# An attention and MLP block in split float32: seven-product pairs moved to tiles 4 and 10, totals taken one bank at a time

## The chip, the cores and the metric

The kernel runs on one core of a Trainium2 chip. The metric is the device time of one execution in microseconds (us); of several timed runs the median counts. Engines: TensorE (PE, its weight loads PEld), VectorE (DVE), ScalarE (ACT), GpSimd (POOL) and SyncE (SP, which issues the weight transfers).

## The reference, cut to what matters

One transformer block on 256 tokens of width 2048 in float32. The stages around the change:

```python
h = h + (g_mla * y_mla + g_fox * y_fox) @ w_out[l]
hn = rmsnorm(h, mlp_norm[l])
u = jnp.square(jax.nn.relu(hn @ w_up[l]))      # 2048 -> 8192
h = h + u @ w_down[l]                          # 8192 -> 2048
return rmsnorm(h, final_norm)
```

Before them come one combined input projection, latent attention and forgetting attention, which the change leaves alone.

## The kernel before, in words

**Split products.** Each float32 operand is held as a high part (rounded to the format that TensorE multiplies) and a low part (the rest). A product is three matmuls into one PSUM bank: high x high, high x low, low x high (`three_passes`, L695 to L699). Every matmul has a 128 x 128 stationary block and 512 moving columns. The activations are stationary, the weights moving.

**The weight stream.** All weights arrive as 456 units of 128 x 1024 (512 KB) in the order of use. A ring of four slots holds them raw, another ring of four holds the high and low parts. For unit u SyncE issues the load when unit u-4 has been split (L521); ScalarE rounds it to the high part when TensorE has used unit u-4 (L941, `unit_used`); VectorE subtracts to get the low part (L1190, `unit_split`). ScalarE and VectorE take units strictly in order, and between units the other work that the list `DUE` puts there (`make_due`, L186). `due[u]` is worked off after unit u has been split. A wait in one such piece of work holds all later units on that engine.

**The up product.** `w_up` is taken in two parts of 4096 columns; each part is an up stage (four groups) and a down stage (four groups). A group of the up stage gives 1024 hidden columns (two chunks of 512) for both blocks of 128 tokens: 16 tiles of depth 128, one unit each, into four banks (bank 2c + tb for chunk c and token block tb). An ordinary tile is 4 x 3 matmuls. Two pairs of tiles in each group are done by seven products in place of eight (`seven_products`, L709), as in Strassen's scheme: sums of activations (`sums_hl`) times sums of weights (`wsum_hi`, `wsum_lo`) and plain blocks. Four of the seven go to banks 4 to 7, three directly to banks 1, 0 and 2. `SEVEN = (0, 6)` names the first tile of each pair, so the pairs are tiles 0, 1 and 6, 7. Before splitting the pair's first unit VectorE forms the weight sums out of both raw units (L1200, L1203, L1204), ScalarE rounds them (L946, L948) and VectorE subtracts (L1207). The sums of activations are made once, from the turned and scaled rows of w_out's chunks 0 and 1 (`row_sums`, L1210).

**What follows a group.** ScalarE copies bank 4 (`copy_p1`, due at tile 10) and VectorE sums the four products into `hid` (`sum_products`, three operations, due at tile 11). The last two tiles of a group are done bank by bank, so bank 0 is complete first. `totals` (L1236, due two units after the group) adds banks 0 and 1 one at a time and banks 2 and 3 in one operation. `hidden_squares` does ReLU and square on ScalarE for each chunk (L1007, L1009; due 3 and 4 units after the group). `turn_hidden` transposes each chunk in blocks of 32 on VectorE (L1385; due 4 and 6 units after) into the one buffer `blocks`; GpSimd stores that to HBM and loads it back in four transfers (L545, L552). A transpose waits until the transfer before it has been stored. The chunks that come back are split (L1022, L1405; due 13 and 15 units after).

**TensorE's waits at the start of a group.** The pair at tile 0 first writes banks 7, 5, 6 and 4, in twelve matmuls, then waits for banks 0 and 1 to be free, later for banks 2 and 3. Where the group before in those banks is w_out's or down's, "free" means that VectorE has added it to the residual (`resid_done`; L1456 for w_out, L1461 for down). w_out's last chunk is due at tile 2 of part 0's first group, down's last at tile 3 of part 1's first group. In the list for tile 2 the scaling of w_out's chunk 2 (`turned_times_gains`, L1396) stands ahead of the residual addition.

The text calls the tiles of a group k0 to k15 and the two halves of the MLP part 0 and part 1.

Of the kernel before, what the change touches and what calls it, by code (L numbers as in the profile page):

```python
# [74 lines left out]
        self.name, self.g = name, g  # L75


SEVEN = (0, 6)
SUMS = {k: n for n, k in enumerate(SEVEN)}


def make_groups():
# [103 lines left out]
def make_due():  # L186


    due = [[] for _ in range(N_UNITS)]

    def after(unit, what, g):
        due[min(unit + RING, N_UNITS - 1)].append((what, g))

    for gr in GROUPS:
        middle = gr.u0 + gr.units // 2 - 1
        if (gr.name, gr.g) in SCORES_IN:
            after(middle, "scored", SCORES_IN[gr.name, gr.g])
        if gr.name == "y_fox" and gr.g >= 2:
            after(middle, "mixed", 4 + gr.g)
        if gr.name[:2] == "up":  # L200
            due[gr.u0 + 10].append(("p1 copied", gr))
            due[gr.u0 + 11].append(("products summed", gr))
            due[gr.last + 2].append(("totals", gr))
            for c in range(2):
                piece = Chunk(gr.name, 2 * gr.g + c)
                piece.of, piece.c = gr, c
                due[gr.last + 3 + c].append(("hidden", piece))
                due[gr.last + 4 + 2 * c].append(("hidden turns", piece))
                due[gr.last + 13 + 2 * c].append(("u turned", piece))
            continue  # L210
        if gr.name in ("y_mla", "w_out"):
            if gr.name == "w_out":
                after(gr.last + TURN_UNITS["w"] - 1, "h back", gr)
            after(gr.last + TURN_UNITS[gr.name[0]], {"y": "m turned", "w": "h turned"}[gr.name[0]], gr)
        if gr.name == "fq" and gr.g == 0:
            for later, what in ((2, "x norm"), (3, "latent norms"), (6, "keys rotated"), (9, "cq back"),
                                (10, "cq turned"), (14, "keys back"), (15, "keys turned"), (17, "forget exp"),
                                (18, "forget sums")):
                after(gr.u0 + later, what, gr)
        if gr is GROUPS[-1]:  # L220
            continue
        later = {("fq", 0): 5, ("fq", 1): 4, ("ukv_k", 0): 2, ("w_out", CHUNKS - 1): -1}.get((gr.name, gr.g), 0)
        after(gr.last + later - (gr.units == 1), "group", gr)
        if gr.name == "gates" and gr.g < 4:
            after(gr.last, "mixed", gr.g)
        elif gr.name == "gates" and gr.g == 7:
            after(gr.last, "mixed", 4)
        elif gr.name == "y_fox" and gr.g == 0:
            after(gr.last, "mixed", 5)
        elif gr.name in ("fq", "uq_nope"):  # L230
            after(gr.last + later + 8, "queries turned", gr)
        elif gr.name == "uq_rope":
            after(gr.last + 8, "queries rotated", gr)
# [51 lines left out]
def program(nc, stream, x_t, x_n, consts, gains, final_gain, cum_rows, prob_rows, turn_rows, out_n):  # L285
# [83 lines left out]
    with ctx:  # L369
# [260 lines left out]
        def _(pe):  # L630
            def wait_for_banks(gr):
# [2 lines left out]
                if had is None:  # L634
                    return
                if had.name[:2] == "up":
                    pe.wait_ge(totals_done, 3 * had.n + (2 if gr.pair == 0 else 3))
# [63 lines left out]
            def double_group(gr, tile, before_unit):  # L701
# [4 lines left out]
                def weights(k, c):  # L706
                    return lambda part: hl[:, slot_of(gr.unit[k]), part, c * WIDE:c * WIDE + WIDE]

                def seven_products(k):  # L709

                    n, one = SUMS[k], SUMS[k] == 0
# [5 lines left out]
                    if one:  # L717
                        pe.wait_ge(products_summed, gr.n)
                    pe.wait_ge(wsum_split, 2 * SEVEN_AT[gr.u0 + k] + 1)
                    three_passes(7, sum_rows(2), sum_weights(1), one, last)  # L720
                    three_passes(5, sum_rows(0), sum_weights(0), one, last)
                    pe.wait_ge(wsum_split, 2 * SEVEN_AT[gr.u0 + k] + 2)
                    three_passes(6, sum_rows(1), sum_weights(2), one, last)
                    pe.wait_ge(unit_split, gr.unit[k] + 1)
                    three_passes(4, rows(k, 0), weights(k, 0), one, last).then_inc(seven_summed, 1)
                    if one:
                        if gr.before.name == "w_out":
                            pe.wait_ge(resid_done, RESID0["w_out"] + gr.before.g + 1)
                        elif gr.before.name[:2] == "up":
                            pe.wait_ge(totals_done, 3 * gr.before.n + 2)  # L730
                        else:
                            pe.wait_ge(resid_done, RESID0[gr.before.name] + gr.before.g + 1)
                    three_passes(1, rows(k + 1, 1), weights(k, 1), one, False).then_inc(unit_used, 1)
                    pe.wait_ge(unit_split, gr.unit[k + 1] + 1)
                    three_passes(0, rows(k + 1, 0), weights(k + 1, 1), one, False)
                    if one:
                        if gr.before_right.name[:2] == "up":
                            pe.wait_ge(totals_done, 3 * gr.before_right.n + 3)
                        else:
                            pe.wait_ge(resid_done, RESID0[gr.before_right.name] + gr.before_right.g + 1)  # L740
                    three_passes(2, sum_rows(3), weights(k + 1, 0), one, False).then_inc(unit_used, 1)

                BANKS = [(0, 0), (1, 0), (0, 1), (1, 1)]
                k = 0
                while k < gr.units - 2:
# [4 lines left out]
                        continue  # L750
                    pe.wait_ge(unit_split, gr.unit[k] + 1)
                    for tb, c in BANKS:
                        done = three_passes(2 * c + tb, rows(k, tb), weights(k, c), (k, tb, c) == (2, 1, 1), False)
                    done.then_inc(unit_used, 1)
                    k += 1
                before_unit(k)
                for tb, c in BANKS:
                    for i in range(k, gr.units):
                        pe.wait_ge(unit_split, gr.unit[i] + 1)
                        done = three_passes(2 * c + tb, rows(i, tb), weights(i, c), False, i == gr.units - 1)  # L760
                    if c == 0:
                        done.then_inc(block_left, 1)
                done.then_inc(unit_used, 2)

# [147 lines left out]
        def _(act):  # L912
# [89 lines left out]
            def hidden_squares(piece):  # L1002

                d, c = piece.of.n, piece.c
                act.wait_ge(totals_done, 3 * d + 2 + c)
# [88 lines left out]
            for u in range(N_UNITS):  # L1094
# [4 lines left out]
                for what, g in DUE[u]:  # L1099
# [25 lines left out]
                        forget_exp()  # L1125
                    elif what in ("m turned", "h turned", "u turned"):
                        turned_to_hi(g)
                        if what == "h turned" and g.g < len(SEVEN):
                            row_sums_to_hi(g.g)
                    elif what == "p1 copied":  # L1130
                        copy_p1(g)
                    elif what == "hidden":
# [27 lines left out]
        def _(dve):  # L1160
# [48 lines left out]

            def row_sums(gr):  # L1210

                n, back = gr.g, by_token(turned[:, SPLIT_NO[gr.name, gr.g] % 2])
# [23 lines left out]
            def totals(gr):  # L1236

                dve.wait_ge(products_summed, gr.n + 1)
                dve.wait_ge(block_left, 2 * gr.n + 1)
                nc.vector.tensor_tensor(hid[:, 1], bank[:, 0], hid[:, 1], ALU.add).then_inc(totals_done, 1)  # L1240
                dve.wait_ge(block_left, 2 * gr.n + 2)
                nc.vector.tensor_tensor(hid[:, 2], bank[:, 1], hid[:, 2], ALU.subtract).then_inc(totals_done, 1)
                dve.wait_ge(unit_used, gr.last + 1)
                nc.vector.tensor_tensor(hid[:, 3:5], bank[:, 2:4], hid[:, 3:5], ALU.add).then_inc(totals_done, 1)  # L1244

            def turn_hidden(piece):

# [230 lines left out]
            for u in range(N_UNITS):  # L1478
# [4 lines left out]
                for what, g in DUE[u]:  # L1483
# [35 lines left out]
                        turn_blocks(g, query_rows[:].rearrange("p b h r -> p b (h r)"))  # L1519
                    elif what == "h back":  # L1520
                        turned_times_gains(g)
                        if g.g < len(SEVEN):
                            row_sums(g)
                    elif what in ("m turned", "h turned", "u turned"):
                        turned_to_lo(g)
                        if what == "h turned" and g.g < len(SEVEN):
                            row_sums_to_lo(g.g)
# [94 lines left out]
```

## Time and profile before

| | |
|---|---|
| timed runs, median of 3 | 1294.25 us (1293.98 to 1296.37) |
| profiled execution, its own time | 1288.84 us |
| its span, first to last instruction | 1287.0 us |
| TensorE busy | 1262.4 us, 98% |
| TensorE weight loads busy | 1043.5 us, 81% |
| VectorE busy | 848.8 us, 66% |
| ScalarE busy | 640.6 us, 50% |
| GpSimd busy | 138.0 us, 11% |
| granted TensorE clock, mean | 0.998 |
| chain that ended last | TensorE 78%, VectorE 11%, transfers 6%, issue 2%, ScalarE 2% |

Matmuls overlap: a record of 512 columns lasts 389 ns, yet one starts about every 227 ns while the engine has work. A gap between two starts is therefore longer by about 0.16 us than the idle time in the record. The first matmuls after a gap are a little slower too: the second starts some 0.34 us after the first.

### The profile page before, as it was taken

How to read it: one execution, taken by the hardware profiler on the slowest of the kernel's cores; microseconds unless marked ns; L12 is line 12 of the kernel's file. 1: busy time of each engine (PE TensorE's matmuls, PEld its weight loads, DVE VectorE, ACT ScalarE, POOL GpSimd, SP SyncE). 2: the span in 40 equal slices, each digit the busy share in tenths (PEclk: the TensorE clock that was granted, in tenths of full speed). 3: DMA queues.
4: the chain of work that ended last, by engine and by line, in shares of the span. 5: the costliest groups of instructions: out<-in, count | busy, mean ns of one | idle time of the engine just before them, and what ended most of it. 6: DMA issues, size and time to landing. Idle time of an engine off the chain costs nothing.

```text
span 1287.0 us, 14484 instructions
## 1 busy us (share of the span) xinstructions
PE 1262.4 (98%) x5618; PEld 1043.5 (81%) x5618; DVE 848.8 (66%) x889; ACT 640.6 (50%) x748; POOL 138.0 (11%) x239
## 2 busy tenths in 40 slices
PE   9999999999999999999999999999999999999997
PEld 7888888888888888877877778888888877788886
DVE  6676567546776676688888775444667887654544
ACT  6654345444555444445555654333445556453443
POOL 0122001004211111100101110000001011100000
PEclk9999999999999999999999999999999999999999
DMA  9698756756976788767678777666566767866563
GB/s 338 238 306 281 243 181 218 222 191 205 286 237 213 241 271 265 247 194 239 215 232 245 246 231 239 192 194 192 192 196 213 242 226 253 286 203 212 195 190 123
DMA packets 83141, 293.90 MB, mean 228 GB/s; under 512 B 11320, under 2 KB 12416, under 8 KB 82432
## 3 DMA queue, kind: packets, MB, share of 16 engines
q1 hardware_dynamic: 67536, 243.04, 57.9%
q0 software_dynamic: 14528, 48.00, 12.2%
q10 hardware_dynamic: 1008, 1.92, 0.4%
q8 instruction: 45, 0.74, 0.2%
q14 instruction: 24, 0.20, 0.0%
HBM read 269.45 MB, written 23.47 MB: 228 GB/s over the span
## 4 chain that ended last, share of the span: by engine, by line
PE 78%; DVE 11%; DMA 6%; issue 2%; ACT 2%; POOL 0%; DVEq 0%; POOLq 0%; ACTq 0%
PE bank L651 65%; DVE hl L1190 4%; PE bank L697 4%; PE bank L699 3%; PE bank L698 3%; DMA raw<-weights 3%; DMA turn_rows<-blocks 2%; DVE wsum_lo L1207 1%; ACT hl L941 1%; DVE wsum L1200 1%; DVE blocks L1385 1%; DVE wsum L1203 1%; DVE raw L1204 1%; PE bank L822 1%; ACT hid L1007 0%
## 5 line engine op out<-in xcount | busy, mean ns | idle before, releaser
L1190 DVE TENSOR_TENSOR hl<-raw,hl 128x1024 fp32r<-128x1024 f32 x451 | 547.2, 1230 | 364.4 <-ACT hl L941 364.3
L941 ACT ACTIVATE hl<-raw 128x1024 fp32r<-128x1024 f32 x451 | 470.5, 1056 | 477.0 <-PE bank L651 376.8
L651 PE MATMUL bank<-hl,u_hl 128*128 128x512 f32 x1536 | 348.8, 389 | 2.6 <-DVE hid L1244 2.6
L651 PE MATMUL bank<-hl,x_hl 128*128 128x512 f32 (+1 forms) x1536 | 344.8, 385 | 0.0
L651 PEld LDWEIGHTS bank<-hl,u_hl 128*128 128x128 f32 x1536 | 288.1, 188 | 63.3 <-DVE hid L1244 3.5
L651 PEld LDWEIGHTS bank<-hl,x_hl 128*128 128x128 f32 x1536 | 284.1, 188 | 56.7 <-DVE hl L1181 0.4
L697 PE MATMUL bank<-hl,hn_hl 128*128 128x512 f32 x432 | 168.9, 391 | 4.5 <-DVE resid L1456 3.2
L699 PE MATMUL bank<-hl,hn_hl 128*128 128x512 f32 x432 | 168.1, 389 | 0.0
L698 PE MATMUL bank<-hl,hn_hl 128*128 128x512 f32 x432 | 168.1, 389 | 0.0
L697 PEld LDWEIGHTS bank<-hl,hn_hl 128*128 128x128 f32 x432 | 81.1, 188 | 24.1 <-DVE resid L1456 3.7
L699 PEld LDWEIGHTS bank<-hl,hn_hl 128*128 128x128 f32 x432 | 81.1, 188 | 17.0
L698 PEld LDWEIGHTS bank<-hl,hn_hl 128*128 128x128 f32 x432 | 81.1, 188 | 16.6
L651 PE MATMUL bank<-hl,m_hl 128*128 128x512 f32 x384 | 87.4, 389 | 0.0
L651 PEld LDWEIGHTS bank<-hl,m_hl 128*128 128x128 f32 x384 | 72.0, 188 | 15.2 <-DVE hl L1190 0.3
L545 POOL DMA_DIRECT2D turn_rows<-blocks x35 | 19.7, 564 | 567.0 <-DVE blocks L1385 566.7
L552 POOL DMA_DIRECT2D turned<-turn_rows x96 | 52.7, 555 | 100.7 <-DMA turn_rows<-blocks 95.9
L946 ACT ACTIVATE wsum_hi<-wsum 128x1024 fp32r<-128x1024 f32 x16 | 17.0, 1062 | 75.2 <-DVE wsum L1200 75.2
L651 PE MATMUL bank<-hl,o_fox 128*128 128x512 f32 x192 | 45.1, 392 | 0.0
L651 PE MATMUL bank<-hl,o_mla 128*128 128x512 f32 x192 | 43.7, 389 | 0.0
L651 PEld LDWEIGHTS bank<-hl,o_mla 128*128 128x128 f32 x192 | 36.0, 188 | 7.5
L651 PEld LDWEIGHTS bank<-hl,o_fox 128*128 128x128 f32 x192 | 35.6, 188 | 7.3
L969 ACT ACTIVATE prob<-prob,cols 128x128 f32<-128x128 f32 (+1 forms) x32 | 14.2, 444 | 31.9 <-DVE cols L1352 31.9
(188 smaller groups left out, 786.3 us busy)
## 6 DMA issues: line engine op xcount, KB each, us to landing
raw<-weights SPq DMA_DIRECT2D x454, 512.0 KB, 4.3
turn_rows<-blocks POOLq DMA_DIRECT2D x34, 512.0 KB, 3.7
turned<-turn_rows POOLq DMA_DIRECT2D x96, 128.0 KB, 4.9
prob_rows<-prob_blocks POOLq DMA_DIRECT2D x8, 384.0 KB, 2.7
prob_t<-prob_rows POOLq DMA_DIRECT2D x32, 96.0 KB, 5.8
turned_h<-turn_rows POOLq DMA_DIRECT2D x20, 128.0 KB, 4.6
x_rows<-x_n POOLq DMA_DIRECT2D x2, 1024.0 KB, 9.0
resid<-x_n POOLq DMA_DIRECT2D x1, 2048.0 KB, 8.2
```

What stands on the lines that cost most here:

```text
L545: pool.dma_start(turn_rows[n % 2, :, 0:4 * run], blocks[:, 0:4 * run]).then_inc(blocks_stored, 16)
L552: pool.dma_start(back[32 * q:32 * q + 32].rearrange("p a k b j -> p a (k b j)"), turn_rows[n % 2, :, run * q:run * q + run].rearrange("(a ...
L651: return nc.tensor.matmul(bank[:, gr.pair + tb, 0:gr.cols], tile[:, k, x_part, tb * P:tb * P + P], w, start=k == 0 and not x_part and not ...
L697: nc.tensor.matmul(bank[:, to], rows(0), w(0), start=first, stop=False)
L698: nc.tensor.matmul(bank[:, to], rows(0), w(1), start=False, stop=False)
L699: return nc.tensor.matmul(bank[:, to], rows(1), w(0), start=False, stop=last)
L822: nc.tensor.matmul(bank[:, 6, hh * T:hh * T + T], v[:, 0, cs], prob_t[n % 2][:, :, hh, 0:2].rearrange("p a k j -> p k a j"), start=True, s ...
L941: nc.scalar.activation(hl[:, slot, 0], raw[:, slot], ACT.Copy).then_inc(unit_hi, 1)
L946: nc.scalar.activation(wsum_hi[:, 0:2], wsum[:, 0:2], ACT.Copy).then_inc(wsum_rounded, 1)
L969: nc.scalar.activation(prob[:, hh, piece], prob[:, hh, piece], ACT.Exp, bias=cols[:, 1, c:c + 1], accum_out=cols[:, 2, c:c + 1]).then_inc( ...
L1190: nc.vector.tensor_tensor(hl[:, slot, 1], raw[:, slot], hl[:, slot, 0].bitcast(F32), ALU.subtract).then_inc(unit_split, 1)
L1200: nc.vector.tensor_tensor(wsum[:, 0:2], raw[:, a, WIDE:].unsqueeze(1).broadcast_to([P, 2, WIDE]), raw[:, a:b + 1, 0:WIDE], ALU.add).then_i ...
```

## The change

- The pairs of seven products are tiles 4, 5 and 10, 11 instead of 0, 1 and 6, 7. Their row sums now come from w_out's chunks 1 and 2 (`IN_CHUNK`).
- The copy of bank 4 and the summing of the products are due at tiles 14 and 15 instead of 10 and 11.
- TensorE waits for each bank at its first use in a group, through `begin`, which also sets the matmul's start flag.
- `totals` adds each of the four banks by itself, each when it is complete; `totals_done` counts four for a group instead of three, and `block_left` three instead of two.
- The hidden chunks' ReLU and square are due one unit earlier (2 and 3 units after the group). The transposes are due 3 and 7 units after it instead of 4 and 6, so that four units lie between the two. The splits of what comes back are due 12 and 15 units after instead of 13 and 15.

The core of the diff:

```diff
-SEVEN = (0, 6)
+SEVEN = (4, 10)
 SUMS = {k: n for n, k in enumerate(SEVEN)}
+IN_CHUNK = {k // 4: n for n, k in enumerate(SEVEN)}
...
-            due[gr.u0 + 10].append(("p1 copied", gr))
-            due[gr.u0 + 11].append(("products summed", gr))
+            due[gr.u0 + SEVEN[-1] + 4].append(("p1 copied", gr))
+            due[gr.u0 + SEVEN[-1] + 5].append(("products summed", gr))
             due[gr.last + 2].append(("totals", gr))
...
-                due[gr.last + 3 + c].append(("hidden", piece))
-                due[gr.last + 4 + 2 * c].append(("hidden turns", piece))
-                due[gr.last + 13 + 2 * c].append(("u turned", piece))
+                due[gr.last + 2 + c].append(("hidden", piece))
+                due[gr.last + 3 + 4 * c].append(("hidden turns", piece))
+                due[gr.last + 12 + 3 * c].append(("u turned", piece))
...
+                def begin(to):
+
+                    first = to not in begun
+                    begun.add(to)
+                    if first and to >= 4:
+                        pe.wait_ge(products_summed, gr.n)
+                    elif first:
+                        had = (gr.before, gr.before_right)[to // 2]
+                        if had.name[:2] == "up":
+                            pe.wait_ge(totals_done, 4 * had.n + to + 1)
+                        else:
+                            pe.wait_ge(resid_done, RESID0[had.name] + had.g + 1)
+                    return first
...
-                        done = three_passes(2 * c + tb, rows(i, tb), weights(i, c), False, i == gr.units - 1)
-                    if c == 0:
+                        done = add_to(2 * c + tb, rows(i, tb), weights(i, c), i == gr.units - 1)
+                    if 2 * c + tb < 3:
                         done.then_inc(block_left, 1)
...
-                        if what == "h turned" and g.g < len(SEVEN):
-                            row_sums_to_hi(g.g)
+                        if what == "h turned" and g.g in IN_CHUNK:
+                            row_sums_to_hi(IN_CHUNK[g.g])
...
-                dve.wait_ge(block_left, 2 * gr.n + 1)
+                dve.wait_ge(block_left, 3 * gr.n + 1)
                 nc.vector.tensor_tensor(hid[:, 1], bank[:, 0], hid[:, 1], ALU.add).then_inc(totals_done, 1)
-                dve.wait_ge(block_left, 2 * gr.n + 2)
+                dve.wait_ge(block_left, 3 * gr.n + 2)
                 nc.vector.tensor_tensor(hid[:, 2], bank[:, 1], hid[:, 2], ALU.subtract).then_inc(totals_done, 1)
+                dve.wait_ge(block_left, 3 * gr.n + 3)
+                nc.vector.tensor_tensor(hid[:, 3], bank[:, 2], hid[:, 3], ALU.add).then_inc(totals_done, 1)
                 dve.wait_ge(unit_used, gr.last + 1)
-                nc.vector.tensor_tensor(hid[:, 3:5], bank[:, 2:4], hid[:, 3:5], ALU.add).then_inc(totals_done, 1)
+                nc.vector.tensor_tensor(hid[:, 4], bank[:, 3], hid[:, 4], ALU.add).then_inc(totals_done, 1)
```

## Rows read from the trace of the kernel before

**Rows 1.** Windows: length, then PE, PEld, DVE, ACT, POOL busy (count), clock, DMA share, GB/s
```profile
755.49:929.70 174.21, 174.21 (x768) 144.26 (x769) 92.04 (x80) 74.86 (x72) 5.50 (x10) 1.00 0.63 202
...
1105.63:1279.80 174.17, 174.17 (x768) 144.07 (x768) 89.62 (x84) 77.69 (x87) 5.51 (x10) 1.00 0.62 199
```

**Rows 2.** Timeline of PE: start, duration in us, instruction, count [idle before <- releaser]
```profile
1.32 4.54 PE L846 MATMUL bank<-kr_low 128*128 128x256 f32 x10 [1.32 <-POOL kr_low L534]
...
572.70 1.07 PE L651 MATMUL bank<-hl,m_hl 128*128 128x512 f32 x4
574.60 0.47 PE L697 MATMUL bank<-wsum_hi,sums_hl 128*128 128x512 f32 x1 [0.83 <-DVE wsum_lo L1207]
...
580.85 0.50 PE L697 MATMUL bank<-hl,hn_hl 128*128 128x512 f32 x1 [3.25 <-DVE resid L1456]
...
755.49 0.73 PE L651 MATMUL bank<-hl,u_hl 128*128 128x512 f32 x2 [1.32 <-DVE hid L1244]
...
933.62 0.50 PE L697 MATMUL bank<-hl,hn_hl 128*128 128x512 f32 x1 [1.01 <-DVE resid L1461]
...
1033.46 0.47 PE L697 MATMUL bank<-wsum_hi,sums_hl 128*128 128x512 f32 x1 [2.11 <-DVE wsum_lo L1207]
```

**Rows 3.** Waits of PE over the span: us in total, times, longest
```profile
PE bank L697 <- DVE wsum_lo L1207: 9.2, 6, 2.7
```

**Rows 4.** Timeline of DVE from a group's end to its second pair
```profile
1016.13 0.68 DVE L1240 TENSOR_TENSOR hid<-bank,hid 128x512 f32<-128x512 f32 x1
...
1017.33 1.21 DVE L1244 TENSOR_TENSOR hid<-bank,hid 128x1024 f32<-128x1024 f32 x1
...
1021.72 1.24 DVE L1385 STREAM_TRANSPOSE blocks<-hid 128x1024 f32<-128x1024 f32 x1
...
1028.38 1.25 DVE L1385 STREAM_TRANSPOSE blocks<-hid 128x1024 f32<-128x1024 f32 x1 [2.45 <-DMA turn_rows<-blocks]
1029.54 1.18 DVE L1200 TENSOR_TENSOR wsum<-raw 128x1024 f32<-128x1024 f32 x1
...
1033.83 2.35 DVE L1190 TENSOR_TENSOR hl<-raw,hl 128x1024 fp32r<-128x1024 f32 x2
```

**Rows 5.** Timeline of ACT over the same group's ReLU and square
```profile
1017.44 1.06 ACT L1007 ACTIVATE hid<-hid 128x1024 f32<-128x1024 f32 x1 [0.64 <-DVE hid L1242]
1018.53 1.06 ACT L1009 ACTIVATE hid<-hid 128x1024 f32<-128x1024 f32 x1
1019.50 1.04 ACT L941 ACTIVATE hl<-raw 128x1024 fp32r<-128x1024 f32 x1
```

**Rows 6.** Timeline of DVE, the first of the three operations on the products
```profile
999.79 0.69 DVE L1230 TENSOR_TENSOR hid<-bank,hid 128x512 f32<-128x512 f32 x1
```

**Rows 7.** Timeline of DVE and ACT at the starts of part 0 and part 1
```profile
578.38 1.29 DVE L1396 TENSOR_TENSOR turned<-turned,gain 128x512 f32<-128x512 f32 x2
579.58 1.21 DVE L1456 TENSOR_TENSOR resid<-resid,bank 128x1024 f32<-128x1024 f32 x1
...
932.16 1.40 DVE L1461 SCALAR_TENSOR_TENSOR resid<-bank,rstd_col,resid 128x512 f32<-128x512 f32 x2
...
929.93 1.06 ACT L941 ACTIVATE hl<-raw 128x1024 fp32r<-128x1024 f32 x1 [1.66 <-PE bank L651]
```

**Rows 8.** DMA issues in 683.0:683.5, 674:676 and 563:567, count, KB, us to landing
```profile
raw<-weights SPq DMA_DIRECT2D x1, 512.0 KB, 3.5
...
raw<-weights SPq DMA_DIRECT2D x2, 512.0 KB, 5.8
...
raw<-weights SPq DMA_DIRECT2D x3, 512.0 KB, 8.6
```

**Rows 9.** One of the four row-sum operations: duration ns min/median/max, first and last start
```profile
L1216 DVE TENSOR_TENSOR sums<-turned x2: 292/293/294, 547.3 to 553.6; 128x128 f32<-128x128 f32 x2
```

**Rows 10.** Windows around the longest gap and after the last matmul
```profile
579.00:582.50 3.50, 1.65 (x7) 1.39 (x8) 3.04 (x4) 1.64 (x5) 0.00 (x0) 1.00 0.82 280
...
1280.10:1287.00 6.90, 0.00 (x0) 0.00 (x0) 3.00 (x8) 2.43 (x6) 0.00 (x0) 0.65 0.54 202
```

More of the change, by code:

```diff
@@ L636, in wait_for_banks @@
                 if had.name[:2] == "up":
-                    pe.wait_ge(totals_done, 3 * had.n + (2 if gr.pair == 0 else 3))
+                    pe.wait_ge(totals_done, 4 * had.n + gr.pair + 2)
                 elif had.name in ("keys", "fq") and gr.name[0] == "u":
@@ L707, in weights, with add_to @@
                     return lambda part: hl[:, slot_of(gr.unit[k]), part, c * WIDE:c * WIDE + WIDE]
+                begun = set()
+                def begin(to):
[10 more added lines that the diff above has]
+                    return first
+                def add_to(to, rows, w, last=False):
+                    return three_passes(to, rows, w, begin(to), last)
                 def seven_products(k):
-                    n, one = SUMS[k], SUMS[k] == 0
+                    n = SUMS[k]
                     last = n == len(SEVEN) - 1
@@ L716, in seven_products @@
                         pe.wait_ge(sums_split, n + 1)
-                    if one:
-                        pe.wait_ge(products_summed, gr.n)
                     pe.wait_ge(wsum_split, 2 * SEVEN_AT[gr.u0 + k] + 1)
-                    three_passes(7, sum_rows(2), sum_weights(1), one, last)
-                    three_passes(5, sum_rows(0), sum_weights(0), one, last)
+                    add_to(7, sum_rows(2), sum_weights(1), last)
+                    add_to(5, sum_rows(0), sum_weights(0), last)
@@ L722, in seven_products @@
                     pe.wait_ge(wsum_split, 2 * SEVEN_AT[gr.u0 + k] + 2)
-                    three_passes(6, sum_rows(1), sum_weights(2), one, last)
+                    add_to(6, sum_rows(1), sum_weights(2), last)
                     pe.wait_ge(unit_split, gr.unit[k] + 1)
[L725 to L732, printed above, removed]
@@ L733, in seven_products @@
-                    three_passes(1, rows(k + 1, 1), weights(k, 1), one, False).then_inc(unit_used, 1)
-                    pe.wait_ge(unit_split, gr.unit[k + 1] + 1)
[L735 to L740, printed above, removed]
@@ L741, in seven_products @@
-                    three_passes(2, sum_rows(3), weights(k + 1, 0), one, False).then_inc(unit_used, 1)
+                    add_to(4, rows(k, 0), weights(k, 0), last).then_inc(seven_summed, 1)
+                    add_to(1, rows(k + 1, 1), weights(k, 1)).then_inc(unit_used, 1)
+                    pe.wait_ge(unit_split, gr.unit[k + 1] + 1)
+                    add_to(0, rows(k + 1, 0), weights(k + 1, 1))
+                    add_to(2, sum_rows(3), weights(k + 1, 0)).then_inc(unit_used, 1)
                 BANKS = [(0, 0), (1, 0), (0, 1), (1, 1)]
@@ L752, in double_group @@
                     for tb, c in BANKS:
-                        done = three_passes(2 * c + tb, rows(k, tb), weights(k, c), (k, tb, c) == (2, 1, 1), False)
+                        done = add_to(2 * c + tb, rows(k, tb), weights(k, c))
                     done.then_inc(unit_used, 1)
@@ L1004, in hidden_squares @@
                 d, c = piece.of.n, piece.c
-                act.wait_ge(totals_done, 3 * d + 2 + c)
+                act.wait_ge(totals_done, 4 * d + 2 + 2 * c)
                 z = hid[:, 1 + 2 * c:3 + 2 * c]
@@ L1210, in row_sums @@
             def row_sums(gr):
-                n, back = gr.g, by_token(turned[:, SPLIT_NO[gr.name, gr.g] % 2])
+                n, back = IN_CHUNK[gr.g], by_token(turned[:, SPLIT_NO[gr.name, gr.g] % 2])
                 i = SEVEN[n] - 4 * gr.g
@@ L1521, in _ @@
                         turned_times_gains(g)
-                        if g.g < len(SEVEN):
+                        if g.g in IN_CHUNK:
                             row_sums(g)
@@ L1525, in _ @@
                         turned_to_lo(g)
-                        if what == "h turned" and g.g < len(SEVEN):
-                            row_sums_to_lo(g.g)
+                        if what == "h turned" and g.g in IN_CHUNK:
+                            row_sums_to_lo(IN_CHUNK[g.g])
                     elif what == "products summed":
```

## The prediction

> **What bounds the kernel now.** I began with the table of engines: TensorE is busy for 98% of the span, so only its gaps can be won. Next came the windows. In the two down stages, where TensorE never waits, 768 matmuls take 174.2 us, a pace of 0.2268 us [rows 1]. A group of the up product has 12 x 12 + 2 x 21 = 186 matmuls, both before and after the change, so 42.2 us; a part of four groups has 744 and should take 168.7 us. Part 0 begins where w_out's last matmuls end (572.70 + 4 x 0.2268 = 573.6) and ends where down begins at 755.5: 181.9 us [rows 2]. Part 1 goes from 929.7, the end of the first down stage, to 1105.6, the start of the second: 175.9 us [rows 1]. So 13.1 + 7.2 = **20.3 us** are lost in the up stages, and this is all that the change can touch.
>
> TensorE's timeline gives the sizes [rows 2]:
> - At the start of part 0 1.1 us before the first pair, then 3.5 us for the residual of w_out's last chunk (the matmul at 580.85): 4.7 with the slower restart.
> - At the start of part 1 the same wait is 1.3 us (933.62), short because twelve matmuls into banks 4 to 7 (2.7 us) come before the first that needs bank 0 or 1.
> - At the end of each part 1.6 us until VectorE has added banks 2 and 3 together (755.49: 1.32 idle, and 0.27 between a pace and a record's end, restart included).
> - The rest, 20.3 - 4.7 - 1.3 - 3.2 = **11.1 us**, lies inside the groups, almost all at the second pair (tile 6), waiting for the lower halves of its weight sums, 9.2 us of idle time with the 0.8 of part 0's start in it [rows 3]. The timeline of VectorE says why [rows 4]: it transposes the first chunk at 1021.72, and the second only at 1028.38, since the block buffer is still being stored; the pair's weight sums queue behind it at 1029.54, and TensorE starts the pair at 1033.46, 3.9 us later [rows 2].
>
> **The change part by part.** Let T be the moment at which TensorE may start a group, times in us from T, tiles k0 to k15. Durations: splitting to the low half 1.13 when back to back, 1.22 alone; a pair's sums 4.3 from their first operation to the next split, with TensorE able to start 3.9 after the first [rows 2, 4]; ReLU to square 1.09, square to the next rounding 0.97, and a rounding of 1.06 before its split [rows 5]; the three operations on the seven products 2.6 (0.72 from one to the next, and a last one like the first total of 1.2) [rows 6].
>
> (a) *The wait before the second chunk's transpose goes.* It now stands at k6 and not k5; the first chunk's transpose is at about 3.5, the second at 14.7, and today the second can start 6.7 after the first [rows 4]. The block buffer is free long before. What is late next is the first pair, now k4.
>
> (b) *Totals one bank at a time.* Bank 3 is complete at T, seen 0.2 later; the last addition takes 0.68 instead of 1.21, so the fourth total is there at 0.9. It is 4 x 0.68 against 2 x 0.68 + 1.21 of VectorE, 0.1 us more with the overlap, hidden. At the end of a part the gap falls from 1.6 to 1.05: 2.1 us in all instead of 3.2.
>
> (c) *A wait for each bank, with ordinary tiles first.* The twelve matmuls that covered the totals now come at k4. Bank 0 is wanted at 0, bank 1 at 0.7, bank 2 at 1.4, bank 3 at 2.0. Inside a part this is free if VectorE begins the totals before -0.74. Behind a waiting matmul stand all of TensorE's later ones. Banks 4 to 7 are asked for at k4, long after the previous products were summed: nothing.
>
> (d) *Start of part 1.* Rounding (929.93), split, two residual additions (932.16) until 933.56, then TensorE at 933.6 [rows 2, 7]. None of that chain gets shorter, and bank 0 is wanted at 929.7: the gap is 3.9, with the slow restart **4.0** instead of 1.3.
>
> (e) *Start of part 0.* Without weight sums the splits of tiles 0 and 1 go ahead. Tile 2's load is issued at about 564.8 and takes 8.6 [rows 8], so it is in at 573.4; rounding and split end at 575.8. Behind it VectorE has the gains of chunk 2 (1.2 to the next operation), then, new here, that chunk's row sums, because tile 10 lies in it (four operations at 0.29, 1.2 in all [rows 9]), then the residual addition, 1.2 [rows 7]: 579.4. TensorE wanted bank 0 at 573.6. The gap is 5.9, with restart **6.0** instead of 4.7. Tile 4's row sums are taken at chunk 1, long before.
>
> (f) *Inside a part, ordinary boundary.* I walked the queues. ScalarE now runs the first chunk's ReLU after the second total (-1.2 at -1.8 of the first): ReLU -0.5, square 0.6, rounding k2 1.6, second ReLU 2.5, square 3.6, rounding k3 4.6 to 5.6; VectorE splits k3 to 6.9, sums for k4 from 7.0, TensorE can start the pair at **10.9**. It wants to at 4 x 2.72 = 10.9. So the new place has no slack to speak of, but no stall either. From there: k4 split from 11.3, k5 12.5, k6 13.6, transpose 14.7, k7 to 17.1; each is before TensorE's need (k6 at 15.7, k7 at 18.4). The load of k11 is issued at 17.1; alone a load takes 3.5, beside a transpose's copies 5.8 [rows 8]; I take 4.5, as the store is on its way and the four loads back are not: 21.6, sums from 21.9, TensorE can start the second pair at 25.8, wants at 26.6. Then k10 and k11 are split until 28.6. The totals of this group begin 18.7 us after these sums: 5.6 to the end of k10's split, 3.5 for k14's load, ScalarE 0.95 for k14, 0.95 for the turned chunk and 0.54 for the copy of bank 4 before it rounds k15 (1.1), VectorE 1.13 for k15, 2.6 for the products, 1.13 and 1.15 for the next two tiles. That is 40.6, or -1.6 for the next group. That is where I began, -1.8: the loop closes at about 42.4 against TensorE's 42.2. I take **1.5 us** for the six boundaries in all, with bounds 0 and 11.1 (what they cost now, nearest row) or more (rival 2).
>
> (g) *The clock.* The granted clock is 1.00 around the gap of 3.6 us, yet after the last matmul it falls to its lower level, 1.2 of 2.4 GHz: over the 6.9 us from 1280.1 on it is 0.65 in the mean, so 4.8 us were at half and it fell 2.1 us after the engine stopped [rows 10]. The new gap of 5.9 is beyond both, the one of 3.9 is nearest to the 3.6 that did not lower it. I take one fall. Its price: matmuls twice as long while it lasts; no row has this for 512 columns, so I bound it by 0 and, as an estimate, the 4.5 us that the engine spent on its warm-ups from 1.32 on [rows 2], taken at half rate, 2.3 us. I take **1.5**.
>
> Sum of what is lost after: 6.0 + 4.0 + 2.1 + 1.5 + 1.5 = 15.1, against 20.3: **5.2 us gained**. The profiled execution took 1288.84 (span 1287.0), so 1283.6 for one like it. The median of the timed runs is 5.4 above it, for which no row has a cause; taking the gain from that, 1294.25 - 5.2 = **1289.1**.
>
> **The rivals.**
> 1. *The starts cost less*, because chains (d) and (e) overlap more, or the clock stays: 1.5 to 3 us better, **1286.5**. For it: the clock stood through 3.6 us. Against it: every link of (d) is a row.
> 2. *VectorE comes to the boundary late* (slower). Today its first total starts at 1016.13 while the group began at 1015.5 (1033.46 less a gap of 2.3 and 15.7 of matmuls), +0.6, harmless behind twelve matmuls [rows 2, 4]. If the loop of (f) stays as late, TensorE waits 0.74 + 0.6 = 1.3, up to 2.2, at bank 0, plus a restart of 0.1. What would make it so is the load of k11: with 6.9 instead of 4.5 the loop takes 44.8. Six boundaries at 1.4 to 2.3 are 8.4 to 13.8; lost 22 to 27.4, **1298**. The whole gain is gone from about 1.1 us a boundary (6.7 in six) onwards.
> 3. *A mild form of the same*: a load of 5.5, 1 us over at each boundary but the first slack: 4.5 in place of 1.5, **1292.1**.
> 4. *The clock falls at both starts*, and for the whole 4.5 us: 2 x 2.3 instead of 1.5, **1292.2**. The fall after only 2.1 us of rest speaks for it, the gap of 3.6 at full clock against it. The Trainium skill, "TensorE: Matmul & The Clock Gate", Part 1, says that the half-rate state is the default and that only activity lifts the engine out of it; by that rule both new gaps would be followed by slow matmuls. The trace agrees for the end of the kernel and disagrees for the 3.6 us gap.
> 5. *Nothing changes at the second pair*: the wait would have been for the weight sums themselves. Against it: 2.45 us of waiting for the block buffer stand right before one of them [rows 4]. Too small to list alone.
>
> **How the numbers follow.** Forecast 0.45 (own range 1287 to 1291.5), rival 1 0.12, rival 2 0.13, rival 3 0.14, rival 4 0.16. About 0.2%, 2.6 us, can be told from no change, so faster means below 1291.7. The forecast gives faster 0.43, rival 1 0.12, rivals 3 and 4 some 0.04 each: 0.63. Same: most of 3 and 4, 0.23 with a little of the forecast and of 2. Slower 0.14. The range leaves out the far halves of rivals 1 and 2: 1285 to 1298.
>
> **What would show it.** Right: no transpose of a hidden chunk waits for a store; TensorE waits about 6 us at part 0's start and 4 at part 1's, both ended by a residual addition; 1.05 at the ends; the up stages last 168.7 + 9 and 168.7 + 6. Step (f) is wrong if totals start later than -0.74 or waits for the low weight sums stay over 0.5 us at k4 or k10; (g) if the granted clock is 1.00 through part 0's start. The forecast fails if six boundaries cost over 4 us.

## The result, and the profile after

The changed kernel takes 1289.32 us in the median of five runs (1287.14 to 1290.53), the kernel before 1294.41 (1293.98 to 1296.37). The ratio is 0.9946 with a 95% interval of 0.9922 to 0.9970: 0.5% faster, as forecast (1289.1). Its profiled execution took 1289.71 with a span of 1287.9.

The two profiled executions do not show this gain: 1288.84 before, 1289.71 after. The one before was among the fastest of that kernel; of 75 later executions only one was faster (1288.43 to 1302.81, median 1294.75). One execution of e5, 1307.68 us, over 1.5% above that kernel's fastest, counts as slow and is left out of e5's numbers. Now the profile of the changed kernel. Its windows come first: length, then busy time and count of PE, PEld, DVE, ACT and POOL, granted clock, DMA share, GB/s. The first and third are the up stages, the second a down stage, the last two the time behind the two long gaps.

```profile
573.59:752.96 179.37, 172.11 (x746) 140.34 (x745) 151.69 (x160) 101.00 (x110) 19.21 (x35) 0.99 0.69 230
752.96:927.17 174.21, 174.21 (x768) 144.20 (x768) 88.05 (x75) 73.43 (x70) 5.48 (x10) 1.00 0.63 207
927.17:1106.54 179.37, 173.43 (x746) 140.94 (x745) 143.32 (x145) 97.76 (x103) 16.46 (x30) 0.98 0.67 220
577.90:581.60 3.70, 3.64 (x9) 2.91 (x10) 2.49 (x3) 3.67 (x7) 0.56 (x1) 0.54 0.23 95
931.10:936.60 5.50, 5.45 (x13) 4.32 (x14) 4.16 (x5) 1.69 (x2) 0.00 (x0) 0.51 0.23 89
```

The down stage keeps its pace, 174.21 us as in [rows 1]. Each up stage lasts 179.4 us, so each loses 10.6 over the 168.7 of its matmuls: 21.3 us in all, where I had forecast 15.1. Before, in the first profile, it was 13.1 and 7.2.

What TensorE waited for, over the whole span (us, times, longest), against [rows 3]:

```profile
PE bank L698 <- DVE resid L1465: 4.2, 1, 4.2
PE bank L698 <- DVE resid L1470: 3.8, 1, 3.8
PE bank L698 <- DVE wsum_lo L1214: 3.0, 4, 1.3
PE bank L652 <- DVE hid L1253: 1.7, 2, 0.9
```

The weight sums cost 3.0 instead of 9.2 us of idle time; the two residual additions cost 8.0 instead of 4.3; the last totals of each part 1.7 instead of 2.6. No transpose of a hidden chunk waits for a store any more. The timeline of TensorE at these places, for [rows 2]:

```profile
577.96 0.66 PE L698 MATMUL bank<-hl,hn_hl 128*128 128x512 f32 x1 [4.21 <-DVE resid L1465]
578.42 0.63 PE L699 MATMUL bank<-hl,hn_hl 128*128 128x512 f32 x1
...
691.42 0.47 PE L698 MATMUL bank<-wsum_hi,sums_hl 128*128 128x512 f32 x1 [0.67 <-DVE wsum_lo L1214]
...
735.78 0.47 PE L698 MATMUL bank<-wsum_hi,sums_hl 128*128 128x512 f32 x1 [1.26 <-DVE wsum_lo L1214]
...
752.96 0.50 PE L652 MATMUL bank<-hl,u_hl 128*128 128x512 f32 x1 [0.89 <-DVE hid L1253]
...
931.15 0.76 PE L698 MATMUL bank<-hl,hn_hl 128*128 128x512 f32 x1 [3.82 <-DVE resid L1470]
```

A record of 0.63 us instead of 0.39, and a granted clock of 0.54 and 0.51 in the windows behind 577.9 and 931.1, are the clock at its lower level, 1.2 GHz.

### The profile page after: what moved, and what is told of

It is laid out like the page before. It is cut to its first block, busy times and chain, and to the rows that moved or that the text cites. A ratio compares the mean times of both kernels' runs of the same rounds, so it can differ in the third digit from the quotient of the medians.

```text
span 1287.9 us, 14508 instructions
## 1 busy us (share of the span) xinstructions
PE 1266.0 (98%) x5618; PEld 1047.1 (81%) x5618; DVE 851.1 (66%) x897; ACT 641.0 (50%) x748; POOL 137.7 (11%) x239
## 4 chain that ended last, share of the span: by engine, by line
PE 76%; DVE 12%; DMA 5%; ACT 3%; issue 3%; DVEq 0%; ACTq 0%
PE bank L652 67%; DMA raw<-weights 5%; DVE hl L1197 4%; PE bank L698 2%; PE bank L699 2%; PE bank L700 2%; ACT hl L948 2%; DVE wsum_lo L1214 2%; DVE wsum L1207 1%; ACT hid L1014 1%; DVE wsum L1210 1%; DVE raw L1211 1%; DVE blocks L1394 1%; PE bank L829 1%; DVE hid L1239 0%
## 5 line engine op out<-in xcount | busy, mean ns | idle before, releaser
L698 PE MATMUL bank<-hl,hn_hl 128*128 128x512 f32 x432 | 170.6, 395 | 8.5 <-DVE resid L1465 4.2
L699 PE MATMUL bank<-hl,hn_hl 128*128 128x512 f32 x432 | 170.0, 394 | 0.0
L700 PE MATMUL bank<-hl,hn_hl 128*128 128x512 f32 x432 | 169.8, 393 | 0.0
L698 PEld LDWEIGHTS bank<-hl,hn_hl 128*128 128x128 f32 x432 | 82.1, 190 | 28.2 <-issue 11.2
L700 PEld LDWEIGHTS bank<-hl,hn_hl 128*128 128x128 f32 x432 | 82.1, 190 | 17.3
L699 PEld LDWEIGHTS bank<-hl,hn_hl 128*128 128x128 f32 x432 | 82.1, 190 | 17.0
```

The source lines that it names most:

```text
L698: nc.tensor.matmul(bank[:, to], rows(0), w(0), start=first, stop=False)
L699: nc.tensor.matmul(bank[:, to], rows(0), w(1), start=False, stop=False)
L700: return nc.tensor.matmul(bank[:, to], rows(1), w(0), start=False, stop=last)
```

## The experiments

All times are medians; the kernel before ran in the same jobs: 1294.7 beside the first four, 1295.1 beside the next four, 1295.7 beside the last four. "Lost" is the length of the two up stages, part 0 and part 1, less 168.7 us each, in the profiled execution. "Slow" counts matmul starts 427 ns apart in them, and not those in the down stages.

| run | median us | ratio to before (95%) | lost, us | slow |
|---|---|---|---|---|
| before, first profile | 1294.4 | | 13.1 + 7.2 | 0 |
| changed | 1289.3 | 0.9946 (0.9922 to 0.9970) | 10.6 + 10.6 | 7 + 12 |
| e1 before again | 1293.1 | 1.0005 (0.9986 to 1.0024) | 17.5 + 7.7 | 19 + 0 |
| e2 transpose alone | 1279.0 | 0.9885 (0.9865 to 0.9905) | 7.5 + 2.7 | 7 + 0 |
| e3 pairs back | 1297.1 | 1.0023 (1.0006 to 1.0040) | 14.7 + 11.3 | 7 + 14 |
| e4 early additions | 1281.8 | 0.9907 (0.9886 to 0.9928) | 9.9 + 5.6 | 14 + 0 |
| e5 transpose at tile 8 | 1296.8 | 1.0018 (0.9992 to 1.0043) | 7.9 + 17.5 | 6 + 18 |
| e6 e4 with e5 | 1290.0 | 0.9957 (0.9935 to 0.9980) | 5.7 + 5.9 | 0 |
| e7 e2, early additions | 1279.8 | 0.9889 (0.9871 to 0.9908) | 8.2 + 1.4 | 0 |
| e8 e7, single totals | 1278.4 | 0.9866 (0.9844 to 0.9887) | 7.0 + 2.0 | 0 |
| e9 e5, return later | 1297.9 | 1.0006 (0.9989 to 1.0023) | 14.1 + 12.7 | 12 + 7 |
| e10 e6, return later | 1287.8 | 0.9941 (0.9920 to 0.9961) | 9.0 + 7.5 | 0 |
| e11 e8, return later | 1276.5 | 0.9862 (0.9843 to 0.9882) | 8.3 + 0.9 | 0 |
| e12 e3, ReLU later | 1279.2 | 0.9881 (0.9860 to 0.9902) | 9.0 + 3.6 | 12 + 0 |

**e1, the kernel before once more.** No edit.

> The kernel before, run again and profiled again. Theory A: its median (1294.4) is 5.5 us above its first profiled execution (1288.84) because in most executions the granted clock falls in the 3.6 us gap at the start of part 0; it did not fall in the profiled one. Then most timed runs show a mean clock of 0.996 to 0.997 in place of 0.998, and a new profile shows slow matmuls (427 ns apart) after the gap in some 2 of 3 cases. One fall costs 1.5 to 2.5 us, so half of the 5.5 at most. Theory B: the clock is the same in all, and the 5.5 us are spread over waits that vary between executions (loads): mean clock 0.998 throughout.

The second profile lost 25.2 us where the first lost 20.3. Here is TensorE after the same gap in part 0, and the clock of the window behind it:

```profile
580.99 0.79 PE L697 MATMUL bank<-hl,hn_hl 128*128 128x512 f32 x1 [3.28 <-DVE resid L1456]
```

```profile
581.00:587.00 6.00, 6.00 (x14) 4.74 (x15) 4.79 (x5) 5.26 (x8) 1.29 (x3) 0.51 0.63 242
```

The gap has the same 3.3 us of idle time as in [rows 2], but the clock fell: 19 starts at 427 instead of 227 ns, in two slow stretches, cost about 4 us, most of the 4.9 us that this profile lost more. So A is right that the first profile was a fortunate one and that the clock falls in most executions: of all 75 later ones eight had a mean clock of 0.998 or more. The clock does not explain the spread, though. Those eight took 1293.2 us on average, 4.4 more than the first profile, and the fastest of the 75 (1288.43) had a mean clock of 0.995. What else varies between executions stays open, since only two of them were profiled.

**e2, the transpose alone.** On the kernel before:

```diff
-due[gr.last + 4 + 2 * c].append(("hidden turns", piece))
+due[gr.last + 4 + 4 * c].append(("hidden turns", piece))
```

> The kernel before with one edit: the second hidden chunk's transpose is due 8 units after its group instead of 6, so it comes after the weight sums of the second pair (tile 6). Theory A (the wait for the block buffer in front of those sums is what costs 11 us inside the groups): TensorE's idle time for the low weight sums falls from 9.2 to under 3 us, the starts stay at 4.7 and 1.3, and the time falls by 6 to 10 us, to 1285 to 1288: more than the whole change gained. Rival B (the loads set the loop, and the weight sums wait for the raw units anyway): under 3 us gained, time 1291 to 1294.

A, and more than its range said: 1279.0, some 15 us less than before, two to three times the gain of the whole change. TensorE's waits:

```profile
PE bank L697 <- DVE resid L1456: 3.3, 1, 3.3
PE bank L651 <- DVE hid L1244: 2.6, 2, 1.3
PE bank L846 <- POOL kr_low L534: 1.3, 1, 1.3
PE bank L697 <- DVE resid L1461: 1.0, 1, 1.0
PE bank L697 <- DVE wsum_lo L1207: 0.6, 1, 0.6
```

Only the start of part 0 is left of the weight sums' row, 0.6 us; inside the groups TensorE does not stop at all. So the 9.2 us of [rows 3], but for the 0.8 at part 0's start, came from the transpose that waited for the block buffer ahead of the sums.

**e3, the pairs back.** On the changed kernel:

```diff
-SEVEN = (4, 10)
+SEVEN = (0, 6)
```

> The changed kernel with the pairs put back to tiles 0 and 6; all else as changed (single totals, a wait for each bank, transposes 3 and 7 units after the group). Theory A (the pairs' new place costs the cover at the starts of the parts): the gaps at the starts fall from 4.6 and 4.2 us to about 3.6 and 1.4 with the clock mostly kept, worth 4 to 7 us at the starts; inside the groups the wait stays small since the second transpose comes after the sums of tile 6: time 1283 to 1287. Rival B (the early pair is worth more than the cover, since the sums at tile 0 come right at the totals): stalls at tile 0 of 0.5 to 1.5 us in six boundaries, time 1289 to 1294.

Neither: 1297.1 is beyond both. At the starts A was right in kind (the two residual waits cost 1.1 and 1.0 us). But a new wait appears in ten places, and the clock fell behind three of its gaps of 2.5 us:

```profile
PE bank L698 <- DVE hl L1197: 11.5, 10, 2.1
```

The timeline of ScalarE at one of them (TensorE resumes at 624.05):

```profile
619.55 1.06 ACT L1014 ACTIVATE hid<-hid 128x1024 f32<-128x1024 f32 x1 [2.67 <-DVE hid L1249]
620.64 1.06 ACT L1016 ACTIVATE hid<-hid 128x1024 f32<-128x1024 f32 x1
621.61 1.04 ACT L948 ACTIVATE hl<-raw 128x1024 fp32r<-128x1024 f32 x1
```

The first chunk's ReLU is now due ahead of tile 2's rounding (621.61), waits there 2.67 us for the totals, and with its square takes 2.1. A pair at tiles 0 and 1 wants tile 2 at 4.8 us, ordinary tiles want it at 5.4. e12 tests this.

**e4, early additions.** On the changed kernel (the sort puts w_out's addition first among the work of tile 2):

```diff
+    first = due[BY["up0", 0].u0 + 2]
+    first.sort(key=lambda item: item[0] != "group")
...
-("w_out", CHUNKS - 1): -1}
+("w_out", CHUNKS - 1): -1, ("down0", CHUNKS - 1): -1}
```

> The changed kernel with the two residual additions at the starts earlier: in part 0 ahead of the scaling and row sums of w_out's chunk 2, in part 1 after tile 2's split instead of tile 3's. Theory A: the gaps shrink from 4.6 to about 2.0 and from 4.2 to about 1.7 us, the granted clock stays at 1.00 through both, so 2.5 + 2.5 us of gap and 1.6 + 2.5 us of slow matmuls go: 9 us, time about 1280 to 1282. Rival B: the time is given back later, since the loop over the loads sets the end of each part: under 3 us gained, 1286.5 to 1289.

A's time: 7.5 us below the changed kernel by the medians, 5 by the two ratios. Part 1 is as A foresaw:

```profile
928.32 0.47 PE L700 MATMUL bank<-hl,hn_hl 128*128 128x512 f32 x1 [1.59 <-DVE resid L1472]
```

```profile
577.50:583.50 6.00, 5.95 (x14) 4.74 (x15) 5.90 (x10) 4.01 (x7) 1.35 (x3) 0.50 0.51 186
926.60:932.00 5.40, 3.81 (x17) 3.08 (x17) 5.17 (x7) 2.20 (x3) 0.00 (x0) 1.00 0.63 190
```

The gap is 2.0 instead of 4.2 and the clock stays at 1.00. In part 0 A was wrong: the gap shrank by 0.5 only, since the load of tile 2 took 9.2 us in place of 7.9, so that VectorE split that tile at 575.05 and not at 573.08, and the clock fell. e6 and later take that addition after tile 1.

**e5, the transpose at tile 8.** On the changed kernel:

```diff
-due[gr.last + 3 + 4 * c].append(("hidden turns", piece))
+due[gr.last + 3 + 6 * c].append(("hidden turns", piece))
```

> The changed kernel with one edit: the second chunk's transpose is due 9 units after its group instead of 7, so at tile 8, after the splits whose weight loads the second pair waits for. In the changed kernel these loads took 5.6 to 6.9 us with the store of that transpose beside them, and TensorE lost 6 us inside the groups. Theory A (store and transpose stand in the loop): the load of tile 11 takes about 1.3 us less and is issued 1.1 us earlier, the six boundaries cost under 2 us in all, time 1284 to 1286. Rival B (the burst of four loads behind the first pair's weight sums is enough by itself): the load stays over 5.5 us, under 2 us gained, time 1287.5 to 1289.5.

By the time both are wrong: 1296.8. By the profile A's mechanism is right. The load of tile 11 is issued 1.1 us after tile 10's (2.2 to 2.8 in the changed kernel) and takes 5.1 to 5.7 us in five of the six boundaries (5.6 to 6.9 there); no matmul waits for weight sums any more, and the last three groups of part 0 lose nothing at all. So store and transpose in the loop were behind what the changed kernel lost inside the groups. The loss came back at another place, in part 1. One load of tile 11, and the new wait:

```profile
raw<-weights SPq DMA_DIRECT2D x1, 512.0 KB, 5.7
...
PE bank L698 <- DVE hl L1197: 4.5, 3, 2.5
```

ScalarE shows why:

```profile
1009.62 1.06 ACT L1029 ACTIVATE u_hl<-turned 128x1024 fp32r<-128x1024 f32 x1 [4.38 <-DMA turned<-turn_rows]
```

The chunk comes back through HBM later than tile 14, where it is due, and every rounding behind it waits; TensorE then stood idle for 1.8 us, until 1013.42.

**e6, e5 and both additions early.**

```diff
-("w_out", CHUNKS - 1): -1}
+("w_out", CHUNKS - 1): -2, ("down0", CHUNKS - 1): -1}
-due[gr.last + 3 + 4 * c].append(("hidden turns", piece))
+due[gr.last + 3 + 6 * c].append(("hidden turns", piece))
```

> The changed kernel with the transpose at tile 8 and both residual additions early (w_out's last chunk after tile 1's split, down's last after tile 2's). Theory A (gaps at the starts, slow matmuls after them and the loop over the loads are all that is lost): gaps about 1.7 us at both starts, granted clock 1.00 through them, boundaries under 2 us: time 1275 to 1278. Rival B (gains do not add, since one bound replaces the other): 1279 to 1282.

Neither: 1290.0, with a wide spread (1282 to 1297). Against e5 the starts are worth 7 to 8 us (gaps of 1.8 and 2.0, no slow matmul behind them), and against e4, which has the early additions too (w_out's one tile later), the time is 8.2 us longer. The profile, taken in the fastest of the twelve executions (1282.2), shows only part of this: idle gaps of 1.8 us at the first pair's sums, 1.2 before a split and 2.2 before part 1's down stage, which is followed by slow matmuls.

**e7, e2 with the early additions.** On the kernel before:

```diff
-due[gr.last + 4 + 2 * c].append(("hidden turns", piece))
+due[gr.last + 4 + 4 * c].append(("hidden turns", piece))
-("w_out", CHUNKS - 1): -1}
+("w_out", CHUNKS - 1): -2, ("down0", CHUNKS - 1): -1}
```

> The kernel before with the second transpose two units later (the single edit that gave 1279.0) and both residual additions early. Theory A: the gap in part 0 falls from 3.4 us to about 1, the one in part 1 from 1.2 to 0, no slow matmuls: 3.5 us less, time 1275 to 1276.5. Rival B (the additions delay the rounding of the next tiles, and the pair at tile 0 gives it back): 1278 to 1279.5.

**e8, e7 with the totals one bank at a time**, with the counts of `block_left` and `totals_done` as in the change:

```diff
-nc.vector.tensor_tensor(hid[:, 3:5], bank[:, 2:4], hid[:, 3:5], ALU.add).then_inc(totals_done, 1)
+nc.vector.tensor_tensor(hid[:, 3], bank[:, 2], hid[:, 3], ALU.add).then_inc(totals_done, 1)
+dve.wait_ge(unit_used, gr.last + 1)
+nc.vector.tensor_tensor(hid[:, 4], bank[:, 3], hid[:, 4], ALU.add).then_inc(totals_done, 1)
```

> The kernel of e7 with the totals taken one bank at a time, each when its bank is complete. Theory A: only the gap at the end of each part shrinks, from 1.48 to 0.95 us: 1.1 us in all, time about 1274.5. Rival B: the extra operation on VectorE delays the next split, and the time stays as in e7 or rises by under 1 us.

e7 is B: 1279.8, nothing gained on e2. The gap for the residual in part 0 fell to 1.3 us start to start and that of part 1 went, but four waits for a split came up in part 0, 2.8 us of idle time, the longest 1.4. e8 has 1278.4, and not the 1274.5 of its theory A; the gap at the ends is 1.17 start to start instead of 1.71, which is A's 1.1 us in the two ends, but between medians whose intervals overlap this cannot be told from nothing.

**e9, e5 with the return later.** The split of the second chunk is due 17 units after its group, not 15, but for the last group of a part.

```diff
-due[gr.last + 12 + 3 * c].append(("u turned", piece))
+due[gr.last + 12 + (3 if gr.g == FF_DOUBLES - 1 else 5) * c].append(("u turned", piece))
```

> The kernel of e5 (changed kernel, second transpose at tile 8) with one more edit: the turned second chunk is split two units later (17 units after its group) except behind a part's last group. In e5 ScalarE waited 4.4 us at tile 14 for the chunk's way back through HBM, and TensorE 2.2 behind it. Theory A (the return is the new wait; without it the loop over the loads is shorter): the wait goes, boundaries cost under 3 us in six, only the last group of a part keeps it; time 1285 to 1288. Rival B (the loads, not the return, hold the engines): under 3 us gained on e5, time over 1294.

**e10, the same diff on e6.**

> The kernel of e6 (second transpose at tile 8, both residual additions early) with the second chunk's split two units later as in e9. Theory A: as e9 without the gaps at the starts and their slow matmuls, 8 us less than e9: 1277 to 1280. Rival B: the spread of e6 (1282 to 1297) stays, median over 1286.

**e11, the same on e8.**

```diff
-due[gr.last + 13 + 2 * c].append(("u turned", piece))
+due[gr.last + 13 + (2 if gr.g == FF_DOUBLES - 1 else 4) * c].append(("u turned", piece))
```

> The kernel of e8 (before, with the second transpose after the second pair's sums, early additions, single totals) with the second chunk's split two units later. Theory A: in e8 ScalarE and VectorE wait some 3 us for this return in each group, which shows at TensorE as small gaps of 0.2 to 1 us at the next group's start; they go, 1 to 3 us gained, 1275.5 to 1277.5. Rival B: that wait lies in slack, time 1278 to 1279.

e9 is B: 1297.9. The wait for the return is gone inside the parts, and another stands in its place. TensorE:

```profile
PE bank L652 <- DVE hid L1253: 5.2, 2, 2.8
...
PE bank L698 <- DVE hid L1247: 3.1, 3, 1.1
```

The second row is my rival 2: the first total comes late, and bank 0 is wanted at once. VectorE shows what stands before it, up to the first total (L1247):

```profile
706.37 1.22 DVE L1197 TENSOR_TENSOR hl<-raw,hl 128x1024 fp32r<-128x1024 f32 x1
707.50 1.22 DVE L1414 TENSOR_TENSOR u_hl<-turned,u_hl 128x1024 fp32r<-128x1024 f32 x1
708.64 1.22 DVE L1197 TENSOR_TENSOR hl<-raw,hl 128x1024 fp32r<-128x1024 f32 x1
709.77 0.68 DVE L1247 TENSOR_TENSOR hid<-bank,hid 128x512 f32<-128x512 f32 x1
```

The split that was put off (L1414, 1.14 us to the next operation) now stands between tiles 0 and 1 of the next group, right ahead of the totals. The three waits in the row come to 1.0 us each; the same split stands there before the down stages too, which is part of the first row. In this group a second thing adds to it: the load of tile 14 goes out at 693.9 while the four loads back of the transpose run (from 692.62 on GpSimd's queue), takes 5.9 us, and ScalarE waits 3.45 us for it. How much each costs was not run apart. So e9 did not test its theory A cleanly: the edit took one wait away and put another in.

e10 gives 1287.8: B by its median, but its spread is 6 us and not that of e6 (the 2.2 between the two medians lies within their intervals). e11 gives 1276.5, in the range of its theory A and the fastest kernel, though not to be told from e8.

**e12, ReLU later.** e3 with

```diff
-due[gr.last + 2 + c].append(("hidden", piece))
+due[gr.last + 3 + c].append(("hidden", piece))
-due[gr.last + 3 + 4 * c].append(("hidden turns", piece))
+due[gr.last + 4 + 4 * c].append(("hidden turns", piece))
```

> The kernel of e3 (changed kernel with the pairs at tiles 0 and 6) with ReLU and square due 3 and 4 units after the group and the transposes 4 and 8, as in e2. It differs from e2 only by single totals and a wait for each bank. Theory A (in e3 the ReLU ahead of the rounding of tile 2 cost 2 to 2.5 us at five of six boundaries, since a pair at tile 0 wants tile 2 at 4.8 us): these waits go, time 1278 to 1280. Rival B (the early pair with a wait for each bank costs by itself): over 1285.

A: 1279.2, and 0.5 us of idle time for a split instead of 11.5. So a wait for each bank and single totals are harmless: with them and early pairs the kernel is as fast as e2. e3's loss was in the list's places, by ScalarE's timeline the ReLU's; e12 moves both transposes by one unit too, and the two were not run apart.

## Why the prediction was right, step by step, and where two errors met

The time came out to 0.2 us, but the sum behind it did not: the changed kernel should have lost 15.1 us and lost 21.3. That the time fits is luck.

- **(a), the wait for the block buffer: right.** It is gone, and e2 shows that it was all of the loss inside the groups.
- **(b), 2.1 us at the ends: measured 2.0** (gaps of 1.28 and 1.21 less the pace of 0.23).
- **(c): right.** No matmul waits for a total inside the groups. The first total of a group begins at 706.13, some 1.4 us before TensorE may start (707.5, by 718.62 less the small gap and 10.9 of matmuls).
- **(d), a gap of 3.9 in part 1: measured 3.98** over the pace (931.15), the chain link by link as foreseen.
- **(e), a gap of 5.9 in part 0: measured 4.37.** The links hold, as this timeline of VectorE for [rows 7] shows, but they begin 1.5 us earlier: tile 2's load was in by 572.0 instead of 573.4. That is one execution; the profiles of e5 and e9, with the same code here, have 5.3 and 6.1.

```profile
573.08 1.23 DVE L1197 TENSOR_TENSOR hl<-raw,hl 128x1024 fp32r<-128x1024 f32 x1 [1.50 <-ACT hl L948]
574.22 1.29 DVE L1405 TENSOR_TENSOR turned<-turned,gain 128x512 f32<-128x512 f32 x2
575.54 0.29 DVE L1223 TENSOR_TENSOR sums<-turned 128x128 f32<-128x128 f32 x1
...
576.60 1.21 DVE L1465 TENSOR_TENSOR resid<-resid,bank 128x1024 f32<-128x1024 f32 x1
```

- **(f), 1.5 us for six boundaries: measured 6.6** (3.5 in part 0, 3.1 in part 1), of it 3.6 at the sums of the second pair. This is the term that was most mis-sized. The loop is the right one; its load was too short. From the chain that ended last, start and length:

```profile
681.04 6.35 DMA raw<-weights
687.39 0.04 DVEq L1206
687.42 0.04 issue
687.47 1.24 DVE wsum L1207
...
724.82 6.92 DMA raw<-weights
...
731.83 1.24 DVE wsum L1207
...
737.40 3.47 DMA raw<-weights
```

  The load of tile 11 takes 5.6, 6.4 and 6.9 us in part 0, where I took 4.5; that of tile 14 takes 3.5, as taken. My loop of 42.4 without its two loads is 34.4; with 6.9 and 3.5 it would be 44.8, and from sums to sums (687.47 to 731.83) it is 44.4. TensorE needs 42.2. By its size that is between rivals 3 and 2: their cause, the load of tile 11, is right, but the waits stand at the second pair's sums, not at the totals. The long load is the last of four issued within 4.6 us behind the first pair's sums, with the transpose's store among them: that store took 7.3 us. e5, where store and transpose come later, has no such wait.
- **(g), one fall of the clock for 1.5 us: two falls, 1.7 and 2.6 us, slow restart included.** Rival 4 in kind: the clock fell behind the gap of 3.9 too. The price was near the estimate at one start and over its bound of 2.3 at the other; the place where the clock holds was wrong. That one gap of 3.6 had kept it proved nothing, as e1 showed: the same gap had it fall.

The terms: 4.4 + 1.7 at one start, 4.0 + 2.6 at the other, 2.0 at the ends, 6.6 inside: 21.3.

The two errors met in the base. I took the gain from the first profiled execution, which I knew to be 5.4 us under the median, and had no row for the cause. Such an execution gained nothing (1288.84 to 1289.71). The second profile of before, near the median, lost 4.9 us more than it, mostly because the clock falls there too (e1). So the median gained 5.1, near the forecast 5.2, of which only the size and not the path was right.

What the change did as a whole: taking the second transpose behind the second pair's sums is worth some 15 us by itself (e2). The move of the pairs, with the ReLU ahead of tile 2 that goes with it, takes 8 to 10 back: the cover of twelve matmuls at the starts, two falls of the clock behind the gaps, and a loop through the loads. The changed kernel with the additions early (e4) wins back 5 to 7.5 of it. With early pairs, the early places of the ReLU and the transposes cost 18 us (e3 against e12). Late pairs with the ReLU in its old place were not run, so the cost of the pairs' place by itself stays open. The fastest kernel is e11, 1276.5 us, 1.4% under before.

## What to carry to other kernels

When a wait vanishes from an in-order queue, move that one piece of work alone first: the other edits of a change can cost more than it and hide it. Before twelve matmuls of cover are moved away from a boundary, look at the boundaries where they covered something else, here the residual additions. And compare a profiled execution with the median before taking a gain from it.

## What the runs showed of the hardware

- The size of a gap did not decide whether the granted clock fell. It fell behind a gap of 3.7 us start to start in one execution and held at one of 3.6 in another of the same kernel (e1 and [rows 2]). In the one profile of e10 it held at 3.72 us and fell at 3.71, before the two down stages (windows as above):

```profile
751.20:757.00 5.80, 5.73 (x25) 4.73 (x26) 3.22 (x4) 5.77 (x6) 0.56 (x1) 1.00 0.33 116
1101.70:1108.00 6.30, 6.22 (x15) 4.87 (x16) 3.63 (x4) 5.60 (x6) 0.56 (x1) 0.50 0.71 263
```

- It fell just behind gaps of 2.5 us in e3 and held at 2.8 in e11 and 3.1 in the first profile of before. In the profiles of e4 and e6 it held at the gaps of 1.8 to 2.0 at the starts. A fall cost 6 to 13 matmul starts at 427 ns instead of 227, that is 1.2 to 2.6 us.
- A weight load of 512 KB took 3.5 us by itself and 6.9 as the last of four and beside a store; the store itself took 3.3 beside one load at a time and 7.3 there.
- The same program's executions on one chip differ by up to 13 us (1289.9 to 1302.8 for before, beside e5 to e8), and e5 and e6 spread by 15 each; e2, e8 and e11, which wait little inside the groups, by 2 to 5.
